# First two modulation vectors as products on TensorE, x loaded ahead of the parameters, first FFN input by two engines

## What is computed

```python
c_act = jax.nn.silu(c)                          # 1 x 1024
for l in range(DEPTH):                          # 2 layers
    mod = c_act @ mod_w[l] + mod_b[l]           # 1024 x 9216 weights
    sh1, sc1, g1, sh2, sc2, g2, sh3, sc3, g3 = jnp.split(mod, N_MOD, axis=-1)
    f = swiglu(modulate(x, sh1, sc1), ffn_in[l, 0], ffn_out[l, 0])
    x = deepnorm_residual(x, f, g1, ln_g[l, 0], ln_b[l, 0], 0.5)
    ...
# modulate(x, shift, scale) = x * (1 + scale) + shift
```

## Time and profile before

| | |
|---|---|
| median of three runs | 2387.88 us (2387.2 to 2388.28) |
| the profiled execution | 2389.0 us, its span 2386.9 us |
| TensorE matmuls | 2273.7 us, 95% |
| VectorE | 1664.8 us, 70% |
| ScalarE | 1190.5 us, 50% |
| share of the last chain on TensorE | 77% |

### The profile page before, as it was taken

One profiled execution on the slowest core, in us unless ns is written; L12 is line 12 of the kernel. 1 busy time (PEld: TensorE's weight loads), 2 busy tenths in 40 slices (PEclk: granted clock), 3 DMA queues, 4 the chain that ended last, 5 costly groups with the idle time before them and its releaser, 6 DMA issues.

```text
span 2386.9 us, 40650 instructions
## 1 busy us (share of the span) xinstructions
PE 2273.7 (95%) x16788; PEld 2152.9 (90%) x16788; DVE 1664.8 (70%) x1725; ACT 1190.5 (50%) x1213; POOL 230.3 (10%) x199
## 2 busy tenths in 40 slices
PE   4999889999999989999999999999999999999999
PEld 4997888799889877899799997999999999799999
DVE  5997786786689976855655569865565546996555
ACT  2443555455455445455355455665355435465534
POOL 0122000010111300000022000012001200001200
PEclk9999999999999999999999999999999999999999
DMA  8996433586569752555545543444545454244453
GB/s 346 352 354 227 164 131 124 204 326 252 196 244 362 283 203 78 197 192 177 185 177 191 177 159 106 159 177 176 187 171 172 181 179 162 102 159 177 176 186 136
DMA packets 75936, 471.53 MB, mean 198 GB/s; under 512 B 8707, under 2 KB 8963, under 8 KB 27580
## 3 DMA queue, kind: packets, MB, share of 16 engines
q1 hardware_dynamic: 53136, 383.80, 44.1%
q0 software_dynamic: 18976, 68.71, 7.8%
q10 hardware_dynamic: 3724, 17.56, 1.9%
HBM read 468.97 MB, written 1.06 MB: 197 GB/s over the span
## 4 chain that ended last, share of the span: by engine, by line
PE 77%; DVE 12%; ACT 6%; DMA 4%; issue 2%; ACTq 0%; DVEq 0%; SPq 0%
PE ab L1824 49%; PE acc L1824 13%; PE acc L1946 9%; DVE wlo L1021 3%; ACT whi L458 2%; DMA raw<-stream 2%; PE mb L2183 1%; DMA par<-params 1%; DVE sc L1635 1%; DMA modmem<-mods 1%; DVE sc L1106 1%; PE acc L2211 1%; PE mb L1824 0%; DVE rstd L1225 0%; DVE x L1222 0%
## 5 line engine op out<-in xcount | busy, mean ns | idle before, releaser
L1824 PE MATMUL ab<-u_hi,whi 128*128 128x256 f32 x3664 | 1053.2, 287 | 26.6 <-DVE u_lo L1203 11.7
L1824 PE MATMUL ab<-u_lo,whi 128*128 128x256 f32 x3664 | 1044.3, 285 | 0.0
L1824 PE MATMUL ab<-u_hi,wlo 128*128 128x256 f32 x3664 | 1043.7, 285 | 0.0
L1021 DVE TENSOR_TENSOR wlo<-raw,whi 128x2048 fp32r<-128x2048 f32 x361 | 826.8, 2292 | 297.3 <-ACT whi L458 295.7
L458 ACT ACTIVATE whi<-raw 128x2048 fp32r<-128x2048 f32 x361 | 688.9, 1910 | 474.1 <-DMA raw<-stream 302.8
L1824 PEld LDWEIGHTS ab<-u_hi,whi 128*128 128x128 f32 x3664 | 710.7, 194 | 42.6 <-issue 28.6
L1824 PEld LDWEIGHTS ab<-u_lo,whi 128*128 128x128 f32 x3664 | 711.2, 194 | 0.3
L1824 PEld LDWEIGHTS ab<-u_hi,wlo 128*128 128x128 f32 x3664 | 710.9, 194 | 0.0
L1824 PE MATMUL acc<-h_hi,whi 128*128 128x256 f32 (+1 forms) x1032 | 293.4, 284 | 4.2 <-ACT sc L835 1.6
L1824 PE MATMUL acc<-h_lo,whi 128*128 128x256 f32 (+1 forms) x1032 | 292.0, 283 | 0.0
L1824 PE MATMUL acc<-h_hi,wlo 128*128 128x256 f32 (+1 forms) x1032 | 292.0, 283 | 0.0
(11 more groups left out here) (330 smaller groups left out, 2062.7 us busy)
## 6 DMA issues: line engine op xcount, KB each, us to landing
raw<-stream SPq DMA_DIRECT2D x365, 1024.0 KB, 4.8
modmem<-mods POOLq DMA_DIRECT2D x128, 512.0 KB, 6.1
sc<-lnrows ACTq DMA_DIRECT2D x5, 1024.0 KB, 4.8
sc<-start ACTq DMA_DIRECT2D x4, 1024.0 KB, 16.4
gateb<-gaterows ACTq DMA_DIRECT2D x6, 512.0 KB, 3.8
hank<-toep POOLq DMA_DIRECT2D x8, 192.0 KB, 3.8
x<-xT ACTq DMA_DIRECT2D x1, 1024.0 KB, 31.2
x<-xn ACTq DMA_DIRECT2D x1, 1024.0 KB, 4.8
```

Source lines behind the costliest of these rows:

```text
L1021: nc.vector.tensor_tensor(wlo[:, n % RAW, :], raw[:, n % RAW, :], whi[:, n % RAW, :].bitcast(F32), ALU.subtract).then_inc(lo_ready, 1)
L1824: ins = nc.tensor.matmul(out, l, r, start=first and i == 0, stop=last and i == 2, skip_group_check=True)
```

## The change

Five edits, all at the start of the program.

VectorE's sums are gone. TensorE multiplies each part as it lands: 16 products of 128x128 (a block of the part's weights as the stationary operand) with one moving column, `cact[:, k]`, added up over k in the 16 columns of `mb`. A part that is used up is counted by `start_used`, and SyncE waits for counts 1, 3, 5 and 7 of it, for stream blocks 4 to 7.

The biases of the two vectors come with `c`, as one load of 24 columns into `small`, so `bcol` and `gcol` do not wait for the parameters. `x` is issued ahead of the parameters. The copy of `mean_r` stands behind the first input, and TensorE waits for it only behind the first block. GpSimd's first modulation loads wait for `x`.

ScalarE makes the pairs 0 and 2 of the first input, VectorE the pairs 1 and 3; `split_lo` of block 4 stands between VectorE's first pair and its first `u_lo`.

```diff
--- before.py
+++ after.py
@@ -120,7 +120,6 @@
         mean_r = nc.alloc_sbuf_tensor_at("mean_r", [P, P], F32R, offset=HANK_AT + 4 * (MODRING + 2) * D + 4 * AT["meanones"][0])
         flip = nc.alloc_sbuf_tensor_at("flip", [P, P], F32R, offset=HANK_AT + 4 * (MODRING + 2) * D + 4 * AT["chunkmask"][0])
         par = sb("par", [P, NPAR])
-        cin = sb("cin", [P, 8])
         cact = sb("cact", [P, 8])
         modc = sb("modc", [P, 48])
         gcol = sb("gcol", [P, 8])
@@ -133,6 +132,7 @@
         wa2s = sc[0:16, 40:42, :].rearrange("p a n -> p (a n)")
         zas = sc[0:16, 42, :]
         scanmask = rstd[:, 1, :]
+        cin, mod_b0 = small[:, 0:8], small[:, 8:24]
         rbs = sb("rbs", [33, 8])
 
         def col(name, i=0, n=1):
@@ -215,8 +215,7 @@
         c_in = sem("c_in")
         start_in = [sem(f"start_in{i}") for i in range(DM - START)]
         cact_ready = sem("cact_ready")
-        startacc = sem("startacc")
-        startsum = sem("startsum")
+        start_used = sem("start_used")
         startcols = sem("startcols")
         mod_in = [sem(f"mod_in{i}") for i in range(MODRING)]
         mod_done = sem("mod_done")
@@ -371,7 +370,7 @@
             for g in range(RAW):
                 sp.dma_start(raw[:, g, :], stream[g]).then_inc(raw_ready[g], 16)
             for g in range(RAW, RAW + START):
-                sp.wait_ge(lo_ready, g - RAW + 1)
+                sp.wait_ge(start_used, 2 * (g - RAW) + 1)
                 sp.dma_start(raw[:, g % RAW, :], stream[g]).then_inc(raw_ready[g % RAW], 16)
 
             with sp.Fori(0, NBLK // RAW - 2) as it:
@@ -404,7 +403,7 @@
             for f in range(3):
                 for v in range(min(vecs_of(f), 5)):
                     early[MODS_AT[f] + DM * min(vecs_of(f), 5) + MODRING + (v if vecs_of(f) > 5 else 0)].append(v)
-            pool.wait_ge(startsum, 1)
+            pool.wait_ge(x_in, 16)
             for i in range(MODK):
                 for v in early[i]:
                     vec_low(v)
@@ -600,7 +599,7 @@
                     ins.then_inc(ua_ready, 1)
                     act.wait_ge(ua_ready, 2 * n + q // 2 + 1)
                     lead(q)
-                    act.wait_ge(ud_ready, 2 * n + q // 2 + 1)
+                    act.wait_ge(ud_ready, 2 * n + q // 2 + 3)
                     lead(q + 1)
                 if n < 4:
                     gate_rows((2, 4, 3, 5)[n])
@@ -950,27 +949,30 @@
                         nc.scalar.activation(h_hi[:, 0:2, :], sc[:, 32:34, :], ACT.Copy).then_inc(phi_ready, 1)
                 b_blocks(1)
 
-            act.dma_start(cin[:], params[:, 0:8]).then_inc(c_in, 16)
+            act.dma_start(small[:, 0:24], params[:, 0:24]).then_inc(c_in, 16)
             for k in range(DM - START):
                 act.dma_start(sc[:, 8 + 8 * k:16 + 8 * k, :].rearrange("p a n -> p (a n)"), start[:, k, :])\
                     .then_inc(start_in[k], 16)
+            act.dma_start(x[:], xT).then_inc(x_in, 16)
             act.dma_start(par[:], params).then_inc(params_in, 16)
-            act.dma_start(x[:], xT).then_inc(x_in, 16)
             act.wait_ge(c_in, 16)
-            nc.scalar.activation(cact[:], cin[:], ACT.Silu).then_inc(cact_ready, 1)
-            act.wait_ge(params_in, 16)
-            nc.scalar.activation(mean_r[:], col("meanones", 0, 128), ACT.Copy).then_inc(mean_ready, 1)
+            nc.scalar.activation(cact[:], cin, ACT.Silu).then_inc(cact_ready, 1)
             split_hi(g[0])
 
             act.wait_ge(startcols, 1)
             act.wait_ge(x_in, 16)
-            for q in range(4):
+            for q in (0, 2):
                 for m in (2 * q, 2 * q + 1):
                     ins = nc.scalar.activation(sc[:, UF + m, :], x[:, m, :], ACT.Identity,
                                                bias=bcol[:, m:m + 1], scale=gcol[:, m:m + 1])
                 link(ins)
-                nc.scalar.activation(u_hi[:, 2 * q:2 * q + 2, :], sc[:, UF + 2 * q:UF + 2 * q + 2, :],
-                                     ACT.Copy).then_inc(uhi_ready, 1)
+                for p in (q, q + 1):
+                    if p > q:
+                        act.wait_ge(ud_ready, q // 2 + 1)
+                    nc.scalar.activation(u_hi[:, 2 * p:2 * p + 2, :], sc[:, UF + 2 * p:UF + 2 * p + 2, :],
+                                         ACT.Copy).then_inc(uhi_ready, 1)
+            act.wait_ge(params_in, 16)
+            nc.scalar.activation(mean_r[:], col("meanones", 0, 128), ACT.Copy).then_inc(mean_ready, 1)
             act.dma_start(x[:].rearrange("p m t -> p (m t)").rearrange("p (t d) -> p t d", t=2), xn).then_inc(x_in, 16)
             split_hi(g[0] + 1)
             gate_rows(0)
@@ -1744,38 +1746,22 @@
 
             nc.vector.memset(rbs[32:33, :], NEG_INF)
             dve.wait_ge(cact_ready, 1)
-            for k in [k for pair in zip(range(START), range(START, DM)) for k in pair]:
-                if k < START:
-                    dve.wait_ge(raw_ready[k], 16)
-                else:
-                    dve.wait_ge(start_in[k - START], 16)
-                for v in range(2):
-                    if k < START:
-                        src = raw[:, k, D * v:D * v + D]
-                    else:
-                        at4 = 8 + 8 * (k - START) + 4 * v
-                        src = sc[:, at4:at4 + 4, :].rearrange("p a n -> p (a n)")
-                    dst = sc[:, 4 * v:4 * v + 4, :].rearrange("p a n -> p (a n)")
-                    if k == 0:
-                        ins = nc.vector.tensor_scalar(dst, src, cact[:, 0:1], None, ALU.mult)
-                    else:
-                        ins = nc.vector.scalar_tensor_tensor(out=dst, in0=src, scalar=cact[:, k:k + 1], in1=dst,
-                                                             op0=ALU.mult, op1=ALU.add)
-                if k < START:
-                    ins.then_inc(lo_ready, 1)
-                    dve.wait_ge(lo_ready, k + 1)
-                elif k < DM - 1:
-                    link(ins)
-                else:
-                    ins.then_inc(startsum, 1)
-            split_lo(g[0])
+            dve.wait_ge(start_used, DM)
+            link(nc.vector.tensor_tensor(bcol[:], mb[:, 1, 0:8], mod_b0[:, 0:8], ALU.add))
+            link(nc.vector.tensor_tensor(gcol[:], mb[:, 1, 8:16], mod_b0[:, 8:16], ALU.add))
+            nc.vector.tensor_scalar(gcol[:], gcol[:], 1.0, None, ALU.add).then_inc(startcols, 1)
+            dve.wait_ge(startcols, 1)
+            dve.wait_ge(x_in, 16)
+            for q in (1, 3):
+                for m in (2 * q, 2 * q + 1):
+                    ins = nc.vector.tensor_scalar(sc[:, UF + m, :], x[:, m, :], gcol[:, m:m + 1], bcol[:, m:m + 1],
+                                                  ALU.mult, ALU.add)
+                ins.then_inc(ud_ready, 1)
+                if q == 1:
+                    split_lo(g[0])
+                u_lo_pairs(q - 1)
+                u_lo_pairs(q)
             dve.wait_ge(params_in, 16)
-            dve.wait_ge(startacc, 1)
-            link(nc.vector.tensor_tensor(bcol[:], mb[:, 1, 0:8], col("mod_b", 0, 8), ALU.add))
-            link(nc.vector.tensor_tensor(gcol[:], mb[:, 1, 8:16], col("mod_b", 8, 8), ALU.add))
-            nc.vector.tensor_scalar(gcol[:], gcol[:], 1.0, None, ALU.add).then_inc(startcols, 1)
-            for q in range(4):
-                u_lo_pairs(q)
             split_lo(g[0] + 1)
             for l in range(DEPTH):
                 ffn(ffn_pair, 2 * l, 3 * l)
@@ -1826,7 +1812,7 @@
                 return ins
 
             def split_ready(n, it=None):
-                pe.wait_ge(lo_ready, at(n + 1, it))
+                pe.wait_ge(lo_ready, at(n - START + 1, it))
 
             def a_block(n, an, it=None, ms=(0, 1)):
 
@@ -2007,6 +1993,9 @@
 
             def ffn_a(behind=None):
                 first_block()
+                if cnt["row"] == 0:
+                    pe.wait_ge(params_in, 16)
+                    pe.wait_ge(mean_ready, 1)
                 if behind is not None:
                     behind()
                 a_static(1)
@@ -2352,15 +2341,19 @@
                 pe.wait_ge(plo_ready, l + 1)
                 b_static(h_hi, h_lo, 1)
 
-            pe.wait_ge(params_in, 16)
-            pe.wait_ge(mean_ready, 1)
-            pe.wait_ge(startsum, 1)
-            for v in range(2):
-                for m in range(DM):
-                    ins = nc.tensor.matmul(mb[:, 1, 8 * v + m:8 * v + m + 1],
-                                           sc[:, 4 * v:4 * v + 4, :].rearrange("p a n -> p (a n)")[:, m * P:m * P + P],
-                                           col("one"), start=True, stop=True)
-            ins.then_inc(startacc, 1)
+            pe.wait_ge(cact_ready, 1)
+            order = [k for pair in zip(range(START), range(START, DM)) for k in pair]
+            for k in order:
+                if k < START:
+                    pe.wait_ge(raw_ready[k], 16)
+                    rows = raw[:, k, :]
+                else:
```

(6 more changed lines are left out.)

## The result

The changed kernel takes **2412.19 us**, the median of four runs (2409.71 to 2414.24), against 2388.08 us for the kernel before, the median of four (2387.2 to 2395.14). The ratio is 1.0099 with a 95% interval of 1.0087 to 1.0111: 1% slower, 24.1 us. By the interval it is 20.8 to 26.5 us. The profiled execution took 2414.24 us, its span 2412.4 us.

A forecast was written before the change was run, and what follows sets the result against it. TensorE, busy for 95% of the span, was taken as the bound, so the start of its dense work counts: columns 23.7 us later plus 0.6 us from the first input, 24.3 us on 2387.88, gives 2412 us, range 2410 to 2416.

The forecast's parts named there:

- The products' price: Start, TensorE: 256 one-column instructions spaced 0.2133 us each, running from 6.25 to 61.0 us.
- The clock: Start, TensorE: one-column products do not raise the clock, so the low spacing of 0.2133 us holds for all 256.
- The first rival: Start, TensorE: the clock rises under the products and the difference disappears, 2388 us; chance 0.11 for within 17 us.
- New G: Start, ScalarE's start on the input: the two columns are there at 61.7 us, 23.7 us later than before.
- G: Start: the point when the two columns are there and ScalarE starts on the input, 38.02 us in the kernel before.
- First input by two engines: First block's input: dense work 3.65 us after the columns, 1.0 later; second block 0.6 us later than before.
- The sum to this point: Start up to the second block: 23.7 us plus 0.6 us, 24.3 us later.
- What hides: Loads behind the start: all landed in either kernel when dense work starts, so the later start wins nothing back.
- Second rival: Start: the landing of x becomes the bound, a gain, with dense work starting from x; 2382.7 us, chance 0.02.

The follow-up runs named there:

- the doubled run: The changed kernel with every product made twice, the second time into 16 columns that nobody reads; 2465.74 us in one run.
- dense matmuls first: The changed kernel with six unread F32 matmuls of 128x512 ahead of the products; 2416.14 us in one run.
- the early split: The changed kernel with VectorE's split_lo of block 4 put back ahead of its wait for the columns; 2406.26 us in one run.

## Why the prediction was right

- **The products' price.** Predicted 0.2133 us for each of 256 instructions, from 6.25 to 61.0. The trace has them from 6.21 to 61.0, and twice as many cost 54.57 us more. That VectorE's sums take "22.4 us" is a slip without effect: 28.5 - 6.19 is 22.3.
- **The clock.** Predicted low throughout, from the one row of 6.96 us. It was low for 55 us here and for 109 us in the doubled run. The first rival, the rise, is out. The prediction had 7 us to judge 55 by; the doubled run and the one with dense matmuls first show that this was the mechanism and no luck. The Trainium skill (TensorE: Matmul & The Clock Gate, What's actually happening) has the clock released by activity; by this case's rows TensorE can be busy without a gap for 109 us and not release it, so what the profile calls busy is not what that rule speaks of. The measurement decides.
- **New G.** Predicted 61.7, 23.7 us later; it is 61.71, 23.69 later than 38.02.
- **First input by two engines.** Dense work predicted 3.65 us after G, measured 3.68, though its terms were off in both directions: the split began 0.65 us after G where the sum has 0.50, and the first `u_lo` 2.20 us behind the split's start where it has 2.29, with 0.83 left for 0.86. That they cancel to 0.03 is luck. The second block was predicted at 0.6 us later relative to G and came at 72.85 - 61.71 = 11.14 for 10.86, 0.3 later, because the clock rose after 3.6 us and not 4.4. The sum to this point: 24.3 predicted, 23.97 measured. That the median came within 0.2 us of 2412 is luck on top: the four runs lie between 2409.71 and 2414.24, and the two traces end 25.5 us apart.
- **What hides.** The stretch from 61 to 66 us shows a DMA share of 0.00: all that may be loaded ahead had landed, and there was nothing in flight that a later start could have used. No idle time was won back: behind its second block TensorE stands idle for 79.0 us, for 75.3 before. The distance does change later, by up to 6 us, but in both directions; some of its steps are where the record of the clock has a low stretch in one of the traces and not in the other (of 6.8 us at 369 us in the trace after), or one of another length. This is within what runs of one kernel differ by (2382.04 to 2395.14 for the kernel before).
- **Second rival.** The prediction let `x` land at 33.7, so that it would be the bound if an instruction took under 0.107 us. This landing was mis-sized: `x` is there at 29.6 (issued at 3.49, 26.1 us to landing), 4.1 us sooner, and the same sum asks for less than (29.6 - 6.25) / 256 = 0.091 us. At the high clock it takes 0.109; the rival was further off than it looked. With VectorE's sums `x` landed at 31 and the columns came at 35, so even there it was not the bound.

What I had not priced is the good part of the change, since it was covered. With VectorE's sums kept, the columns come at 35.02 for 38.02: some 1.8 us by not waiting for the parameters (an estimate: a start at 28.6, behind the last sum, for 30.35), 1.2 by the earlier start on the first vector, which the change doesn't have.

## What to carry to other kernels

A product with a single moving column cost TensorE two instructions with a load of 128x128 weights each, here 0.43 us for a product in F32 at the low clock, and each instruction is spaced like a 256-column matmul of the blocks. Multiply a vector by a large matrix with the matrix as the moving operand (36.2 us here for 61.0), or on VectorE where that engine ends close behind the landing, as it did here. Ahead of dense work that must wait for a short serial stretch, look at which clock that stretch runs at: unread dense matmuls in TensorE's idle time brought 32 small instructions from 6.99 to 3.63 us and the first block from 7.6 to 5.7, worth 3.5 us at the second block and 4.8 in the medians. Before work is moved off an engine, ask what ended last; here it was the parameters' landing, with TensorE's 16 products behind it, and not the sums that were moved.

## What the runs showed of the hardware

- TensorE without a gap in the profile stayed at the low clock for 109 us with one-column F32 products (loads of 333 ns at the median, spacing 0.2133 us), and fell from the high to the low clock 3.8 us into them although it had no idle time (granted clock 1.00, then 0.50).
- One F32 matmul of 128x256 (two instructions) ahead of every four such products (eight instructions) did not hold the clock either: it fell at 18.0 us and stayed at 0.50 for all the products that followed.
- One-column instructions, each with a load of 128x128 F32 weights, are spaced 0.2133 us at the low clock and 0.109 at the high one.
- A moving operand of 512 F32 columns is spaced 3.43 / 8 = 0.43 us an instruction at the high clock, two instructions a matmul, with one column stationary.
- From the first dense instruction of the same first block to the first shorter one, the rise of the clock, it took between 2.7 us (dense matmuls first) and 5.5 us (sums on VectorE); 3.6, 4.4 and 4.8 in others. With the input made in the same way, the second block starts 10.8 us after ScalarE in the first of these and 12.0 in the second, so this alone moves it by 1.2 us.
- Low stretches of the clock differ from run to run: the mean granted clock is 0.984 to 0.989 in eight of the ten profiled runs (0.977 and 0.970 where it fell under the products). Two single runs, of the changed kernel and of the one with the early split, differ by 5.3 us of TensorE's busy time behind the second block, at 0.985 and 0.989.
